# Prompt attention: causal masks taken from TensorE to VectorE and GpSimd

## Chip, cores and metric

The kernel runs on one core of one Trainium2 chip, as one program. The metric is the device time of that program in microseconds (us). Before the change it is 3462.72 us, the median of three runs (3456.31, 3462.72 and 3465.65 us).

## What is computed

One step of a two-layer streaming encoder on 1024 new frames of a prompt and on 8 x 16 frames of running streams with a cache of 2048 frames. The change touches the prompt's attention alone. Cut to that, the reference is:

```python
CHUNK = 64; QBLK = 128; DA_HEADS = 4; SB_HEADS = 8; HEAD_DIM = 64

def diff_attn_block(q, k, v, q_pos, k_pos, lam):
    s = jnp.einsum('bqhmd,bkhmd->mbhqk', q, k).astype(jnp.float32) * (HEAD_DIM ** -0.5)
    mask = (k_pos[None, :] // CHUNK) <= (q_pos[:, None] // CHUNK)
    p = jax.nn.softmax(jnp.where(mask, s, NEG_INF), axis=-1)
    w = p[0] - lam * p[1]
    return jnp.einsum('bhqk,bkhe->bqhe', w.astype(v.dtype), v)

def sb_attn_block(q, k, v, q_pos, k_pos):
    z = jnp.einsum('bqhd,bkhd->bhqk', q, k).astype(jnp.float32) * (HEAD_DIM ** -0.5)
    mask = k_pos[None, :] < q_pos[:, None]
    log_fail = jnp.where(mask, jax.nn.log_sigmoid(-z), 0.0)
    after = lax.cumsum(log_fail, axis=3, reverse=True) - log_fail
    a = jnp.where(mask, jnp.exp(jax.nn.log_sigmoid(z) + after), 0.0)
    return jnp.einsum('bhqk,bkhd->bqhd', a.astype(v.dtype), v)

for blk in range(t // QBLK):          # the prompt: 8 blocks of 128 queries, keys up to the block's end
    lo, hi = blk * QBLK, (blk + 1) * QBLK
    outs.append(fn(q[:, lo:hi], k[:, :hi], v[:, :hi], pos[lo:hi], pos[:hi], *extra))
```

All of it is float32. Only the last 128 x 128 block of keys of each query block needs a mask. For differential attention that is one quadrant: queries 0 to 63 must not see keys 64 to 127. For stick-breaking attention it is the triangle on and above the diagonal.

## The kernel before

The program is a row of phases for each of two layers: projection (with the cached streams' attention), prompt attention (`phase_attention`, prefix `B_`), merge (`D_`), and at the end a final norm. Each phase is written by hand for five engines. An engine has one in-order list of instructions, and semaphores tie the lists together. There is no scheduler: the lists follow one table of steps, `attention_steps()` (L617), which every engine goes through, picking what is its own.

`phase_attention` loops four times (h = 1..4) over pairs of heads of 128 columns; I call one turn a head. A turn has 16 items, n = 0..15: items 0 to 7 are differential attention (DA) and items 8 to 15 stick-breaking (SB), each for one block of 128 queries. An item with b = n % 8 + 1 blocks of keys computes, for m = 0 and 1 (the two maps of DA, the two heads of SB), 128 x 128b scores.

The order of the steps around item n is: `weights(n)`, `scores(n+1, 0)`, `functions(n+1, 0)`, `scores(n+1, 1)`, `functions(n+1, 1)`, `values(n-1)`, `out(n-1)`, then the rounds `prob_t(n)`. In detail:

- Scores (TensorE, L810): b x 128 columns in matmuls of up to 512, 64 rows deep, into PSUM tile `B_sc[:, m]`. Then a mask matmul (L812) adds, as identity times mask, 1e30 to the masked places of the last block. q was scaled by -1/8 beforehand, so a large positive number means masked. The mask matmul ends the group and tells `qk_done`.
- DA: VectorE takes the minimum (L904, `max_ready`), ScalarE the exponential with its sum into `B_ew` (L872, `s_free`), VectorE combines the two maps (L915 to L918, `weights_ready`).
- SB: ScalarE writes sigmoid(z) to `B_fun` (L878) and sigmoid(-z) to `B_ew` (L879, `s_free`). VectorE runs a backward product scan of `B_fun` into `B_surv` (L930) and multiplies `B_ew` by it (L931, `weights_ready`), for u = 0 and then u = 1. `B_fun` has one buffer per u, so the sigmoids of item n+1 wait for the product of item n of the same u.
- `prob_t`: TensorE transposes the weights (L789) in rounds of up to four blocks into two PSUM banks, which ScalarE and VectorE empty in turn into `B_wt` (L856, L891). Values: TensorE multiplies (L831) and VectorE copies the result out (L939, L941).

GpSimd has nothing to do in this phase. The masks come from a constant tile that ScalarE turns into the matmul's type once a phase (L852). PE records of a float32 matmul come in two halves, so x4 at L810 is two matmuls.

## Time and profile before

| | |
|---|---|
| median of three runs | 3462.72 us |
| profiled execution, its own time | 3463.09 us |
| its span | 3461.3 us |
| TensorE matmul busy | 3097.3 us, 89% |
| VectorE busy | 1591.5 us, 46% |
| ScalarE busy | 895.7 us, 26% |
| GpSimd busy | 0.2 us |
| granted TensorE clock, mean | 0.864 of full |
| prompt attention, layers 1 and 2 | about 925 to 1466 us and 2636 to 3178 us |

A busy TensorE here means that records overlap in time, not that the array is at its peak; a granted clock of 0.5 is 1.2 GHz and of 1.0 is 2.4 GHz. The page cuts the span in 40 slices of 86.5 us. In its PEclk row the slices of prompt attention read 7, 6, 6, 7, 6, 6 and 7, 7, 7, 7, 7, 5 (with the edges of the neighbours), where the projection has mostly 9.

### The profile page before, as it was taken

How to read it: one execution, taken by the hardware profiler on the slowest of the kernel's cores; microseconds unless marked ns; L12 is line 12 of the kernel's file. 1: busy time of each engine (PE TensorE's matmuls, PEld its weight loads, DVE VectorE, ACT ScalarE, POOL GpSimd, SP SyncE). 2: the span in 40 equal slices, each digit the busy share in tenths (PEclk: the TensorE clock that was granted, in tenths of full speed). 3: DMA queues.
4: the chain of work that ended last, by engine and by line, in shares of the span. 5: the costliest groups of instructions: out<-in, count | busy, mean ns of one | idle time of the engine just before them, and what ended most of it. 6: DMA issues, size and time to landing. Idle time of an engine off the chain costs nothing. (4 is left out here: it accounts for less than half of the span.)

```text
span 3461.3 us, 52533 instructions
## 1 busy us (share of the span) xinstructions
PE 3097.3 (89%) x21296; PEld 2299.0 (66%) x21296; DVE 1591.5 (46%) x1999; ACT 895.7 (26%) x1537; POOL 0.2 (0%) x4
## 2 busy tenths in 40 slices
PE   4989999999899999879868999999998999997895
PEld 3767677776666656658656767767765666665684
DVE  3634344444154554564356333444432554654553
ACT  2212222222142332320031222222222332333101
POOL 0000000000000000000000000000000000000000
PEclk9999999999876676689989999999997775775898
DMA  6378786676201100054344778767742010012444
GB/s 216 110 242 292 259 296 212 226 239 207 90 28 38 31 28 25 19 202 133 113 148 163 260 260 281 258 221 247 235 154 74 27 46 23 27 28 89 153 145 158
DMA packets 315425, 519.46 MB, mean 150 GB/s; under 512 B 40224, under 2 KB 111008, under 8 KB 315168
## 3 DMA queue, kind: packets, MB, share of 16 engines
q1 hardware_dynamic: 315248, 516.89, 44.4%
q8 instruction: 137, 2.24, 0.3%
q14 instruction: 40, 0.33, 0.0%
HBM read 436.58 MB, written 84.93 MB: 151 GB/s over the span
## 5 line engine op out<-in xcount | busy, mean ns | idle before, releaser
L335 PE MATMUL A_acc<-A_w_hi,A_ht_hi 128*128 128x512 f32 x1728 | 721.5, 418 | 38.1 <-DVE A_w_lo L540 19.1
L335 PE MATMUL A_acc<-A_w_lo,A_ht_hi 128*128 128x512 f32 x1728 | 684.9, 396 | 0.0
L335 PE MATMUL A_acc<-A_w_hi,A_ht_lo 128*128 128x512 f32 x1728 | 683.9, 396 | 0.0
L810 PE MATMUL B_sc<-B_kt,B_qt 64*128 64x512 f32 (+3 forms) x768 | 443.0, 697 | 16.9 <-DVE B_kt L891 15.5
L335 PEld LDWEIGHTS A_acc<-A_w_hi,A_ht_hi 128*128 128x128 f32 x1728 | 331.1, 192 | 134.1 <-issue 26.8
L335 PEld LDWEIGHTS A_acc<-A_w_hi,A_ht_lo 128*128 128x128 f32 x1728 | 330.7, 191 | 74.2
L335 PEld LDWEIGHTS A_acc<-A_w_lo,A_ht_hi 128*128 128x128 f32 x1728 | 332.1, 192 | 57.7
L831 PE MATMUL B_ov<-B_nat_v,B_wt 128*128 128x64 f32 (+1 forms) x1728 | 322.9, 362 | 14.4 <-DVE B_wt L891 14.4
L555 DVE STREAM_TRANSPOSE A_kt<-A_kt 128x2048 f32<-128x2048 f32 x128 | 293.1, 2302 | 76.5 <-DMA A_kt<-in_cache_da_k 69.5
L831 PEld LDWEIGHTS B_ov<-B_nat_v,B_wt 128*128 128x128 f32 x1728 | 305.8, 272 | 20.8 <-issue 20.8
L810 PEld LDWEIGHTS B_sc<-B_kt,B_qt 64*128 64x128 f32 x768 | 163.9, 245 | 156.0 <-issue 137.5
L540 DVE TENSOR_TENSOR A_w_lo<-A_w_raw,A_w_hi 128x1024 fp32r<-128x1024 f32 x96 | 116.5, 1220 | 209.8 <-ACT A_w_hi L432 209.2
L440 ACT ACTIVATE A_stage<-A_acc 128x512 f32<-128x512 f32 x180 | 107.0, 595 | 408.9 <-PE A_acc L335 282.2
L789 PE MATMUL B_tr<-ident,B_ew 128*128 128x128 f32 x864 | 176.8, 359 | 15.2 <-ACT B_wt L856 14.8
L930 DVE TENSOR_TENSOR_SCAN B_surv<-B_fun 128x255 f32<-128x255 f32 (+7 forms) x128 | 172.4, 1347 | 0.0
L482 ACT ACTIVATE A_pt<-A_tr 128x512 f32<-128x512 f32 x128 | 76.3, 596 | 371.6 <-PE A_tr L377 371.6
L812 PEld LDWEIGHTS B_sc<-B_masks_r 128*128 128x128 f32 x256 | 59.1, 231 | 163.8 <-issue 158.2
L432 ACT ACTIVATE A_w_hi<-A_w_raw 128x1024 fp32r<-128x1024 f32 x96 | 100.9, 1058 | 253.7 <-DMA A_w_raw<-in_w_in 138.5
L789 PEld LDWEIGHTS B_tr<-ident,B_ew 128*128 128x128 f32 x864 | 143.4, 194 | 27.3 <-ACT B_wt L856 25.4
L394 PE MATMUL A_ov<-A_v,A_pt 128*32 128x128 f32 x4096 | 140.1, 278 | 21.0 <-ACT A_pt L482 20.9
L872 ACT ACTIVATE B_ew<-B_sc,B_stats 128x256 f32<-128x256 f32 (+7 forms) x128 | 94.8, 740 | 238.5 <-DVE B_stats L904 238.5
L904 DVE TENSOR_REDUCE B_stats<-B_sc 128x1 f32<-128x256 f32 (+7 forms) x128 | 97.0, 758 | 126.7 <-PE B_sc L812 125.3
(132 smaller groups left out, 3287.6 us busy)
## 6 DMA issues: line engine op xcount, KB each, us to landing
A_kt<-in_cache_da_k SPq DMA_DIRECT2D x64, 1024.0 KB, 10.8
A_v<-in_cache_da_v SPq DMA_DIRECT2D x64, 1024.0 KB, 5.8
A_kt<-in_cache_sb_k SPq DMA_DIRECT2D x64, 1024.0 KB, 11.4
A_v<-in_cache_sb_v SPq DMA_DIRECT2D x64, 1024.0 KB, 5.8
A_w_raw<-in_w_in SPq DMA_DIRECT2D x96, 512.0 KB, 4.6
tmp_gates<-A_stage SPq DMA_DIRECT2D x72, 256.0 KB, 4.3
D_gate<-tmp_gates SPq DMA_DIRECT2D x72, 256.0 KB, 3.5
D_w_raw<-in_w_merge SPq DMA_DIRECT2D x32, 512.0 KB, 6.1
```

What stands on the lines that cost most here:

```text
L335: last = nc.tensor.matmul(acc[:, n % 2, :], h[:, k, rows], w[:, slot, cols], start=(k == 0 and j == 0), stop=(k == KC - 1 and j == 2))
L394: last = nc.tensor.matmul(ov[32 * c:32 * c + 32, 0:P], pt[:, slot, j, 32 * c:32 * c + 32], v_in[:, slot, j, c * P:(c + 1) * P], start=Fals ...
L432: nc.scalar.activation(w_hi[:, n % WSLOTS, :], w_raw[:, n % 2, :], ACT.Copy).then_inc(S["w_hi_done"], 1)
L440: ins = nc.scalar.activation(stage[:, n % 2, :], acc[:, n % 2, :], ACT.Sigmoid if gate else ACT.Copy)
L540: nc.vector.tensor_tensor(w_lo[:, n % WSLOTS, :], w_raw[:, n % 2, :], w_hi[:, n % WSLOTS, :].bitcast(F32), ALU.subtract).then_inc(S["w_lo_ ...
L555: nc.vector.transpose(keys, keys).then_inc(S["key_turned"], 1)
L789: last = nc.tensor.transpose(tr[:, r % 2, j * P:(j + 1) * P], block_, ident[:, :])
L810: nc.tensor.matmul(sc[:, m, c:e], qkt[0][m * HD:(m + 1) * HD, qb * P:(qb + 1) * P], qkt[1][m * HD:(m + 1) * HD, c:e], start=True, stop=(e ...
L831: last = nc.tensor.matmul(ov[:, cols], wt[:, u, j * P:(j + 1) * P], nat_v[a][:, j, cols], start=(j == 0), stop=(j == qb))
L872: nc.scalar.activation(e, z, ACT.Exp, scale=-1.0, bias=stats[n % 2][:, m:m + 1], accum_out=stats[n % 2][:, 2 + m:3 + m]).then_inc(S["s_fre ...
L904: nc.vector.tensor_reduce(out=stats[n % 2][:, m:m + 1], in_=sc[:, m, 0:(n + 1) * P], axis=AX.X, op=ALU.min)\
L930: step_(nc.vector.tensor_tensor_scan(out_, in_, in_, 1.0, ALU.mult, ALU.bypass))
```

## The change

The mask matmuls are gone. The last scores matmul of an item tells `qk_done` itself. In DA, VectorE first writes +1e30 into the masked quadrant of PSUM (64 partitions x 64 columns) and waits for its own write before it takes the minimum. In SB, the sigmoids are computed unmasked; GpSimd then sets the masked triangle of `B_fun` to 1 and of `B_ew` to 0 with one `affine_select` each, in place, on 128 x 128, and tells `masked`, on which the scan now waits in place of `s_free`. Also, the loops over h, `Fori` loops of the engines before, are now Python loops: the four heads are written out one after the other, and semaphore values are constants.

```diff
-        masks_r = sbuf("B_masks_r", [P, MASKS], F32R)
-        DSTEPS = 2 * NP_T + 2 * NP_T
+        DSTEPS = 2 * NP_T + 2 * NP_T + 2 * NP_T
...
             def _(pe):
-                pe.wait_ge(S["masks_ready"], 1)
-
-                with pe.Fori(1, NC + 1) as h:
+                for h in range(1, NC + 1):
...
-                                nc.tensor.matmul(sc[:, m, c:e], qkt[0][m * HD:(m + 1) * HD, qb * P:(qb + 1) * P],
-                                                 qkt[1][m * HD:(m + 1) * HD, c:e], start=True, stop=(e < keys))
-                            nc.tensor.matmul(sc[:, m, qb * P:keys], ident_r, mask_r[a], start=False, stop=True).then_inc(S["qk_done"], 1)
+                                last = nc.tensor.matmul(sc[:, m, c:e], qkt[0][m * HD:(m + 1) * HD, qb * P:(qb + 1) * P],
+                                                 qkt[1][m * HD:(m + 1) * HD, c:e], start=True, stop=True)
+                            last.then_inc(S["qk_done"], 1)
...
-                                nc.scalar.activation(fun[:, m, 0:keys], z, ACT.Sigmoid)
+                                nc.scalar.activation(fun[:, m, 0:keys], z, ACT.Sigmoid).then_inc(S["raw_ready"], 1)
                                 nc.scalar.activation(e, z, ACT.Sigmoid, scale=-1.0).then_inc(S["s_free"], 1)
+            @block.gpsimd
+            def _(pool):
+                def before_me(tile, fill):
+                    return nc.gpsimd.affine_select(out=tile, in_=tile, pattern=[[-1, P]], compare_op=ALU.is_gt, fill=fill,
+                                                   base=0, channel_multiplier=1)
+                for h in range(1, NC + 1):
+                    for step in STEPS:
+                        if step[0] == "functions" and step[1] >= NP_T:
+                            _, n, m = step
+                            diag = slice((n - NP_T) * P, (n - NP_T + 1) * P)
+                            pool.wait_ge(S["raw_ready"], h * (2 * NP_T) + (2 * (n - NP_T) + m + 1))
+                            before_me(fun[:, m, diag], 1.0)
+                            pool.wait_ge(S["s_free"], h * (2 * ITEMS) + (2 * n + m + 1))
+                            before_me(ew[n % 2][:, m, diag], 0.0).then_inc(S["masked"], 1)
...
                             dve.wait_ge(S["qk_done"], h * (2 * ITEMS) + (2 * n + m + 1))
+                            step_(nc.vector.memset(sc[0:CHUNK, m, n * P + CHUNK:(n + 1) * P], -NEG))
                             nc.vector.tensor_reduce(out=stats[n % 2][:, m:m + 1], in_=sc[:, m, 0:(n + 1) * P], axis=AX.X, op=ALU.min)\
...
-                                    dve.wait_ge(S["s_free"], h * (2 * ITEMS) + (2 * n + u + 1))
+                                    dve.wait_ge(S["masked"], h * (2 * NP_T) + (2 * (n - NP_T) + u + 1))
```

On TensorE, in the second half of a turn, the order around the scores of the SB item with six blocks of keys was this (`B_tr` are transposes, `B_ov` the values):

```order
L810 MATMUL B_sc<-B_kt,B_qt 128x512
L810 MATMUL B_sc<-B_kt,B_qt 128x256
L812 MATMUL B_sc<-B_masks_r 128x128
L807 REGISTER_ALU
L810 MATMUL B_sc<-B_kt,B_qt 128x512
L810 MATMUL B_sc<-B_kt,B_qt 128x256
L812 MATMUL B_sc<-B_masks_r 128x128
L723 REGISTER_ALU
L825 REGISTER_ALU
L831 MATMUL B_ov<-B_nat_v,B_wt 128x64 x8
L789 MATMUL B_tr<-ident,B_ew 128x128 x5
L723 REGISTER_ALU
L789 MATMUL B_tr<-ident,B_ew 128x128 x5
```

And now TensorE has, at the same place:

```order
L805 MATMUL B_sc<-B_kt,B_qt 128x512
L805 MATMUL B_sc<-B_kt,B_qt 128x256
L805 MATMUL B_sc<-B_kt,B_qt 128x512
L805 MATMUL B_sc<-B_kt,B_qt 128x256
L826 MATMUL B_ov<-B_nat_v,B_wt 128x64 x8
L784 MATMUL B_tr<-ident,B_ew 128x128 x10
```

Nothing has changed places: the mask matmuls and the register instructions are gone, and the second map's scores are followed at once by the values.

On VectorE, at the start of a turn (DA item 0), there stood before:

```order
L903 REGISTER_ALU
L904 TENSOR_REDUCE B_stats<-B_sc 128x1
L903 REGISTER_ALU
L904 TENSOR_REDUCE B_stats<-B_sc 128x1
L914 ISA
L915 RECIPROCAL B_stats<-B_stats 128x2
```

And now, at the same place:

```order
L914 MEMSET B_sc 64x64
L915 TENSOR_REDUCE B_stats<-B_sc 128x1
L914 MEMSET B_sc 64x64
L915 TENSOR_REDUCE B_stats<-B_sc 128x1
L926 RECIPROCAL B_stats<-B_stats 128x2
L927 SCALAR_TENSOR_TENSOR B_stats<-B_stats,nlam 128x1
```

Each minimum has got a write of PSUM ahead of it. GpSimd, which had nothing in the phase, now has this for SB (`B0_` marks layer 1's semaphores):

```order
L877 ISA [waits B0_raw_ready]
L877 AFFINE_SELECT B_fun<-B_fun 128x128
L877 AFFINE_SELECT B_ew<-B_ew 128x128 [waits B0_s_free]
L877 AFFINE_SELECT B_fun<-B_fun 128x128 [waits B0_raw_ready]
L877 AFFINE_SELECT B_ew<-B_ew 128x128 [waits B0_s_free]
```

Four selects an item stand there, the two of u = 0 ahead of the two of u = 1.

## Rows read from the trace of the kernel before

**Rows 1.** Windows: length, busy of PE, PEld, DVE, ACT, POOL; granted clock; DMA, GB/s

```profile
925.00:1466.00 541.00, 506.34 (x1936) 341.03 (x1936) 281.41 (x441) 184.44 (x353) 0.00 (x0) 0.67 0.11 31
2600.00:3180.00 580.00, 535.72 (x2127) 364.41 (x2125) 282.26 (x444) 189.90 (x361) 0.00 (x0) 0.69 0.12 34
```

**Rows 2.** Groups by line, 925 to 1466; busy us, mean ns, idle before and releasers

```profile
L812 PE MATMUL B_sc<-B_masks_r 128*128 128x128 f32 x128 | 50.4, 394 | 0.0
...
L904 DVE TENSOR_REDUCE B_stats<-B_sc 128x1 f32<-128x128 f32 (+7 forms) x64 | 48.5, 758 | 63.9 <-PE B_sc L812 63.4
```

**Rows 3.** Timeline at half clock: start us, us, instruction, idle before it and releaser

```profile
946.48 0.47 PE L812 MATMUL B_sc<-B_masks_r 128*128 128x128 f32 x1
946.88 2.07 PE L810 MATMUL B_sc<-B_kt,B_qt 64*128 64x512 f32 x2
...
948.89 0.47 PE L812 MATMUL B_sc<-B_masks_r 128*128 128x128 f32 x1
949.05 0.97 PEld L831 LDWEIGHTS B_ov<-B_nat_v,B_wt 128*128 128x128 f32 x4
```

**Rows 4.** Timeline at full clock, the same places of a later item

```profile
969.84 0.33 PE L812 MATMUL B_sc<-B_masks_r 128*128 128x128 f32 x1
...
970.10 1.77 PE L810 MATMUL B_sc<-B_kt,B_qt 64*128 64x512 f32 x4
...
971.79 0.33 PE L812 MATMUL B_sc<-B_masks_r 128*128 128x128 f32 x1
971.90 1.20 PEld L831 LDWEIGHTS B_ov<-B_nat_v,B_wt 128*128 128x128 f32 x10
```

**Rows 5.** Windows of one turn, cut where the granted clock changes

```profile
968.00:1012.40 44.40, 40.78 (x220) 27.11 (x218) 31.36 (x52) 22.54 (x44) 0.00 (x0) 1.00 0.17 50
1012.40:1067.00 54.60, 52.34 (x186) 39.60 (x187) 23.54 (x24) 12.54 (x18) 0.00 (x0) 0.50 0.02 5
1067.00:1070.40 3.40, 2.23 (x11) 1.38 (x9) 1.28 (x3) 2.30 (x6) 0.00 (x0) 1.00 0.44 131
1070.40:1101.10 30.70, 30.70 (x72) 16.94 (x71) 14.16 (x31) 8.60 (x24) 0.00 (x0) 0.50 0.16 43
```

**Rows 6.** Timeline, VectorE in DA: a memset, and a minimum at full clock

```profile
925.20 0.06 DVE L883 MEMSET B_surv<- 128x2 f32 x1 [25.68 <-PEq L63]
...
974.94 1.15 DVE L918 SCALAR_TENSOR_TENSOR B_ew<-B_ew,B_stats 128x896 f32<-128x896 f32 x1
...
976.15 1.23 DVE L904 TENSOR_REDUCE B_stats<-B_sc 128x1 f32<-128x1024 f32 x1
```

**Rows 7.** Timeline, VectorE and ScalarE in SB items 11 and 12, full clock

```profile
1000.38 1.21 DVE L930 TENSOR_TENSOR_SCAN B_surv<-B_fun 128x511 f32<-128x511 f32 x1
...
1002.23 1.22 DVE L930 TENSOR_TENSOR_SCAN B_surv<-B_fun 128x511 f32<-128x511 f32 x1
...
1003.08 0.70 ACT L879 ACTIVATE B_ew<-B_sc 128x640 f32<-128x640 f32 x1
...
1005.79 1.48 DVE L930 TENSOR_TENSOR_SCAN B_surv<-B_fun 128x639 f32<-128x639 f32 x1
```

**Rows 8.** Timeline, SB item 8: the shortest operations on 128 x 128

```profile
989.44 0.41 DVE L930 TENSOR_TENSOR_SCAN B_surv<-B_fun 128x127 f32<-128x127 f32 x1
```

**Rows 9.** Timeline: GpSimd's own instructions, one of four alike

```profile
0.24 0.10 POOL L1368 MEMSET const-float32-0.0<- 128x1 f32 x1 [0.24 <-issue]
```

**Rows 10.** Timeline, TensorE where the clock falls and at the next turn's start

```profile
1012.55 1.33 PE L789 MATMUL B_tr<-ident,B_ew 128*128 128x128 f32 x5 [1.59 <-ACT B_wt L856]
...
1063.76 1.91 PE L789 MATMUL B_tr<-ident,B_nat_q 128*128 128x128 f32 x8
```

**Rows 11.** Timeline, TensorE around the place where the clock rises

```profile
965.19 2.02 PE L831 MATMUL B_ov<-B_nat_v,B_wt 128*128 128x128 f32 x8
...
968.14 1.77 PE L810 MATMUL B_sc<-B_kt,B_qt 64*128 64x512 f32 x4
...
973.87 1.98 PE L810 MATMUL B_sc<-B_kt,B_qt 64*128 64x512 f32 x4
```

More of the change, by code:

```diff
@@ L681, in phase_attention @@
     with scope:
-        names = ["masks_ready", "surv_set", "turned", "f_a", "f_v",
+        names = ["surv_set", "turned", "f_a", "f_v", "raw_ready", "masked",
                  "qk_done", "max_ready", "s_free", "weights_ready", "pv_done", "o_ready", "dve_step",
@@ L701, in phase_attention @@
         ident, nlam = const["ident"], const["nlam"]
-        ident_r = masks_r[:, 0:P]
-        mask_r = [masks_r[:, P:2 * P], masks_r[:, 2 * P:3 * P]]
         v_nat_sems = [S["nat_v0"], S["nat_v1"]]
@@ L708, in phase_attention @@
         last_prob = {s[1]: s[-1] for s in STEPS if s[0] == "prob_t"}
-        DSTEPS = 2 * NP_T + 2 * NP_T
+        DSTEPS = 2 * NP_T + 2 * NP_T + 2 * NP_T
         start_phase(nc, [(S["turned"], ROUNDS)] + list(zip(F, COPIES))
-                    + [(S[k], 2 * ITEMS) for k in ("qk_done", "s_free", "weights_ready")] + [(S["max_ready"], 2 * NP_T)]
+                    + [(S[k], 2 * ITEMS) for k in ("qk_done", "s_free", "weights_ready")] + [(S[k], 2 * NP_T) for k in ("max_ready", "raw_ready", "masked")]
                     + [(S[k], ITEMS) for k in ("pv_done", "o_ready")]
@@ L738, in load_slice @@
                 def load_slice(h, dst, src, sem):
-                    cols = bass.ds(h * P - P, P)
+                    cols = slice(h * P - P, h * P)
                     sp.dma_start(dst[:, :, :], src[0:SEQ, cols].rearrange("(t p) c -> p t c", p=P)).then_inc(sem, 16)
@@ L761, in body @@
                             qb = n % NP_T
-                            cols = bass.ds(h * P - P, P)
+                            cols = slice(h * P - P, h * P)
                             sp.wait_ge(S["o_ready"], h * ITEMS + (n + 1))
@@ L770, in _ @@
                 load_slice(1, nat_v[0], dram["v_da"][l], v_nat_sems[0])
-                with sp.Fori(1, NC) as h:
+                for h in range(1, NC):
                     body(h, False)
@@ L851, in _ @@
             def _(act):
-                nc.scalar.activation(masks_r[:, :], const["masks"][:, :], ACT.Copy).then_inc(S["masks_ready"], 1)
-                with act.Fori(1, NC + 1) as h:
+                for h in range(1, NC + 1):
                     def copy(dst, src, scale=None):
@@ L877, in _ @@
                                 act.wait_ge(S["qk_done"], h * (2 * ITEMS) + (2 * n + m + 1))
-                                nc.scalar.activation(fun[:, m, 0:keys], z, ACT.Sigmoid)
+                                nc.scalar.activation(fun[:, m, 0:keys], z, ACT.Sigmoid).then_inc(S["raw_ready"], 1)
                                 nc.scalar.activation(e, z, ACT.Sigmoid, scale=-1.0).then_inc(S["s_free"], 1)
+            @block.gpsimd
[3 more added lines that the diff above has]
+                                                   base=0, channel_multiplier=1)
+                for h in range(1, NC + 1):
+                    for step in STEPS:
[6 more added lines that the diff above has]
+                            before_me(ew[n % 2][:, m, diag], 0.0).then_inc(S["masked"], 1)
             @block.vector
@@ L884, in _ @@
                 dve.wait_ge(S["surv_set"], 1)
-                with dve.Fori(1, NC + 1) as h:
+                for h in range(1, NC + 1):
                     step_ = Steps(dve, S["dve_step"], h * DSTEPS - DSTEPS)
```

## The prediction, made before the changed kernel ran

> **What bounds the kernel now.** I read the windows first, to see which stages the change can reach. Prompt attention is about 541 us in each layer, and in both the TensorE is busy for over nine tenths of it, at a mean granted clock of 0.67 and 0.69 where VectorE is busy for only half [rows 1]. Then I read the groups by line. In layer 1 the 128 mask matmuls have 50.4 us of busy time, with no idle before them; the minimum of DA sat idle for 63.4 us on L812 [rows 2]. So TensorE's list is the spine of the phase, and other engines wait for it. The page's chain of waits ends in the final norm and says nothing of this phase. Third, I cut one turn where the granted clock changes [rows 5]. It is at 2.4 GHz (1.00) for 44.4 us, at 1.2 GHz (0.50) for 54.6, at 2.4 for 3.4 and at 1.2 for 30.7: together 133.1 us, of which 85.3 at the half clock. There TensorE is busy for 52.3 of 54.6 and 30.70 of 30.70 us, and VectorE for less than half. At the full clock VectorE is busy for 31.4 of 44.4 us, and with ScalarE it holds TensorE up at times. The reader should see two regimes: at half clock only TensorE counts; at full clock TensorE, VectorE and ScalarE are nearly level.
>
> **What TensorE is relieved of.** There are 16 items a turn with two masks each, four turns and two layers: 256 mask matmuls. The busy time of one (0.47 us at half clock) includes its latency, so I take the distance between starts. Behind the first map's scores, the mask pushes the next scores back by 946.88 - 946.48 = 0.40 us at half clock [rows 3] and 970.10 - 969.84 = 0.26 at full clock [rows 4]. Behind the second map's, the weight load of the values starts 949.05 - 948.89 = 0.16 us after the mask, and 0.11 at full clock [rows 3, 4]; without the mask it can start where the mask did. One item thus gives 0.56 us at half clock and 0.37 at full clock. In the timeline of the turn, 9 items have their masks at full clock (the first, the last two of DA and the first six of SB) and 7 at half clock (five of DA, the last two of SB). The ceiling is 7 x 0.56 + 9 x 0.37 = 7.25 us a turn, 58 us in eight turns.
>
> **Half clock: all of it is kept.** 7 x 0.56 x 8 = 31 us. VectorE gets two memsets in each of the DA items there. Before, the minimum waited for the mask to end; now it is released a mask earlier and does a memset first. The trace has no write of 64 x 64 to PSUM. From below there is the memset of 2 columns, 0.06 us [rows 6]; from above VectorE's scan of 127 columns, 0.41 us [rows 8]. I take 0.15, nearer the memset, and 0.05 for the wait on its own write, so 0.2 against the 0.4 that the mask took: the exponentials come a little sooner, and nothing is lost. If TensorE did not hold the pace, this cover would be gone, as in the next part.
>
> **Full clock, DA.** The minimum over 1024 columns at 976.15 has no idle before it: VectorE had just finished the product that started at 974.94 and took 1.15 us [rows 6]. With two memsets (0.4 us) on a VectorE that is the later one, the last DA item gives nothing. The one before it had idle time on VectorE and gives its 0.37: 3 us in eight turns. The first item of a turn is a chain of short waits and gives nothing.
>
> **Full clock, SB.** The first two SB items have little for VectorE to do, and TensorE carries the values of DA beside them: 2 x 0.37 x 8 = 6 us. From the third to the sixth, VectorE's round and TensorE's are level: from the scan at 1000.38 to that at 1005.79 is 5.4 us [rows 7], in which scan, product, scan, product, two copies and the wait for the last transposes follow each other. Relief for TensorE gives nothing there. Are the selects late? Sigmoid(-z) of u = 0 ends at 1003.08 + 0.70 = 1003.78, its scan starts at 1005.79 [rows 7]: 2.0 us for at most two selects, and for u = 1 there is as much. What a select takes, no row shows. From below there is GpSimd's memset of one column, 0.10 us [rows 9]. From above I take VectorE's minimum over 1024 columns, eight times the elements: 1.23 us [rows 6]. I take 0.4, from the scan of 127 columns [rows 8]. With 0.4 `masked` comes in time. But the selects do not run beside an idle VectorE. The select on `B_fun` of the next item becomes ready just before 1003.08, in this item's second scan (1002.23 to 1003.45 in item 11), and GpSimd and VectorE then both stream from SBUF. Nothing here shows whether one of them waits. If not, the cost is 0; if VectorE's next instruction waits for one select per map, it is 0.8 us an item. I take half of that, 0.4 us, for four items a turn: 4 x 0.4 x 8 = 13 us lost.
>
> The Trainium skill speaks against the change at this point. "SBUF — State Buffer", section "Who interferes with whom", says that a VectorE instruction with two SBUF inputs and a GpSimd instruction that reads SBUF exclude each other for a whole instruction, whoever started first. The scan and the product here are such instructions; no trace of before can show it, for GpSimd idles. By that rule the cost would be the full 0.8 us an item, 26 us in place of 13.
>
> **Loops and the rest.** The removed loops save a jump and register instructions per turn. TensorE starts the next turn's transposes at 1063.76 [rows 10] while its last values are still draining, so I take 0. The skill's "Runtime: NRT & Kernel Launch", section "Instruction fetch mechanics", would have a taken branch stall on a fetch; TensorE's rows here show no such gap, and by them the sum stays. `masks_r` saves ScalarE one 0.5 us copy per layer, under the wait for the first loads. Projection, merge and final norm are not touched.
>
> **Sum.** 31 + 3 + 6 - 13 = 27 us. The profiled execution took 3463.1 us for a span of 3461.3, and is 0.4 above the median of the runs, so I take 3463.1 - 27 = 3436 us.
>
> **What the sum leaves to chance: where the clock changes.** The clock falls at 1012.4, just as TensorE resumes after 1.59 us of waiting for ScalarE's copy [rows 10]. It rises at 968.0 after a run of values and transposes (from 965.19), where the scores (64 rows deep) had gone before [rows 11]. In each later turn it rises at the same place of the work. Without masks these runs are 0.3 us shorter at half clock and lie elsewhere in time. If the rise comes one item later, the item from 968.14 to 973.87, 5.7 us long, costs up to twice as much.
>
> **Rivals.**
> 1. The clock rises one item late in most turns. [...] Price: 5.2 us less 0.2 for masks dearer there, 5.0 a turn, 40 in eight: 3476 us. If it happens in half the turns, 3456.
> 2. Slower: the selects hold VectorE up. One mechanism, in SB items 3 to 6 at full clock: each item's chain gets two select lengths. With the upper bound of 1.23 us that is 4 x 2 x 1.23 x 8 = 79 us, and the 6 us of the first two SB items are gone too: 3463.1 - 34 + 79 = 3508. It decides from 34 / 64 = 0.53 us a select. For it: every scan waits behind them. Against it: a select has 128 elements per partition, and the row of that size takes 0.41 us [rows 8]. This is also what the skill's rule on SBUF, cited above, would do if a select is long.
> 3. More is gained: selects and scans don't disturb each other, TensorE's relief counts fully at full clock, and the clock falls later. 58 us: 3405 us.
> 4. The masks were hidden all along and nothing changes: 3463 us. For it: TensorE records overlap. Against it: rows 3 show the next start pushed back.
>
> **How the numbers follow.** My forecast, including half of rival 1 and up to the full 0.8 us an item: 0.56, with its own range 3420 to 3456. Rival 1: 0.14. Rival 2: 0.13, mostly under 3508. Rival 3: 0.12. Rival 4: 0.05. For this kernel no change means within 0.3%, 10.4 us, of the median, so 3452.3 to 3473.1. Faster: 0.53 of the forecast's share, all of rival 3, none of the others, 0.65. Same: 0.03 of the forecast, rival 4, most of rival 1 if it is milder than priced, 0.09: together 0.17. Slower: rival 2 and 0.05 of rival 1: 0.18. The range from 3400 to 3480 leaves out most of rival 2 and the edges.
>
> **What would show it.** In the profile after: no second group of matmuls on `B_sc`; scores and values follow at 0.1 us. The AFFINE_SELECT rows' mean: under 0.5 us keeps the sum, above it rival 2. Idle time of the product or scan with releaser POOL in SB tells whether VectorE waits for selects, and a longer mean of the scan that it is slowed. The full-clock stretch of a turn: 44 us as now, or near 38 for rival 1. A turn of 133.1 us should become about 129.7. The forecast is wrong if the memset waits on something longer than its own write (0.2 us), or if the granted clock in prompt attention leaves 0.64 to 0.70.

## The result

| | before | after |
|---|---|---|
| device time, median (range) | 3459.51 us (3450.04 to 3465.65), 4 runs | 3246.38 us (3242.20 to 3249.15), 4 runs |
| profiled execution, its own time and span | 3463.09 / 3461.3 us | 3244.39 / 3242.6 us |
| prompt attention, layers 1 and 2 | 538.7 + 537.5 us | 426.5 + 430.7 us |
| of it at the half clock | 350.9 + 346.3 us | 152.2 + 164.5 us |
| projection, both layers | 915.0 + 910.2 us | 916.5 + 908.1 us |
| merge, both layers | 249.5 + 251.1 us | 251.0 + 249.2 us |

The change makes the kernel 6.15% faster: the ratio is 0.9385, with a 95% interval from 0.9359 to 0.9411. That is 213 us. I had forecast 27 us, with a range down to 3400 us. The prediction was wrong by far, though its sign was right. All of the gain lies in prompt attention: 112.2 + 106.8 = 219 us between the two profiled executions, whose spans are 218.7 apart. (The phases are cut at their first and last record in the trace, the two clock rows add up the stretches at 1.2 GHz inside them.)

From the page of the changed kernel, the busy time of the engines and the clock row:

```profile
PE 2774.6 (86%) x21040; PEld 2118.6 (65%) x21040; DVE 1599.5 (49%) x2127; ACT 890.7 (27%) x1535; POOL 114.0 (4%) x260
PEclk9989999999987988789989999999999878986998
```

Windows of prompt attention in both layers, then of one turn, cut where its clock changes for long (length, busy of PE, PEld, DVE, ACT and POOL, granted clock, DMA):

```profile
925.00:1403.00 478.00, 371.81 (x1912) 272.39 (x1913) 315.78 (x546) 199.92 (x374) 57.15 (x128) 0.81 0.20 59
2525.00:2957.00 432.00, 346.32 (x1808) 252.85 (x1808) 285.39 (x505) 181.83 (x352) 56.69 (x128) 0.81 0.14 40
...
1142.40:1164.30 21.90, 18.02 (x58) 11.70 (x58) 12.31 (x37) 7.87 (x21) 0.00 (x0) 0.50 0.30 82
1164.30:1212.10 47.80, 38.87 (x231) 27.18 (x229) 36.69 (x68) 26.29 (x52) 9.84 (x24) 1.00 0.17 47
1212.10:1249.10 37.00, 30.64 (x168) 24.80 (x169) 22.29 (x22) 11.31 (x16) 4.62 (x8) 0.73 0.02 6
```

The first window takes in 50 us of the merge behind the phase, as the second of [rows 1] takes in 36 us ahead of it; over the phases alone, cut as in the table, the granted clock is 0.82 and 0.81 where it was 0.67 and 0.68. Two things stand out against [rows 1, 5]. One is that clock. The other is that a turn of 106.7 us has 47.8 at the full clock (44.4 before), then 37.0 in which the clock goes up and down at a mean of 0.73, where it stood at 0.50 for 54.6 us. TensorE is now busy for 39 of the 48 us at the full clock: it waits more, and it does not hold the others up as it did.

The place of [rows 3] in the changed kernel, on TensorE at the half clock (start, length, instruction). These are the scores of the DA item with four blocks of keys:

```profile
944.51 2.72 PE L805 MATMUL B_sc<-B_kt,B_qt 64*128 64x512 f32 x4
947.16 0.58 PE L826 MATMUL B_ov<-B_nat_v,B_wt 128*128 128x128 f32 x1
```

And of the kernel before, the two ends of the same place that [rows 3] leave out:

```profile
944.48 2.07 PE L810 MATMUL B_sc<-B_kt,B_qt 64*128 64x512 f32 x2
949.16 0.52 PE L831 MATMUL B_ov<-B_nat_v,B_wt 128*128 128x128 f32 x1
```

The changed kernel's first row explains the result. Before, the first map's matmul began at 944.48, its mask at 946.48, the second map at 946.88, its mask at 948.89 [rows 3], and the values at 949.16: 4.68 us. Now both maps take 947.16 - 944.51 = 2.65 us, at the same clock. Two masks and two gaps can't be 2 us. Each map alone took 2.00 us before (944.48 to 946.48); both together now take 2.65. They run side by side. The trace's single records say the same. This is how many of L805's are under way in two stretches, the second of which begins where the second map does (length, busy of PE and of the weight load with records, granted clock, DMA):

```profile
944.60:945.15 0.55, 0.55 (x1) 0.41 (x2) 0.50 0.00 0
945.15:945.30 0.15, 0.15 (x2) 0.14 (x1) 0.50 0.00 0
```

The first half of the first map's matmul runs to 945.73, and the second map starts in the midst of it, at 945.16. The kernel before has one record (x1) of L810 in either stretch.

Groups by line of the changed kernel, 925 to 1403 (busy us, mean ns, idle before and releasers):

```profile
L805 PE MATMUL B_sc<-B_kt,B_qt 64*128 64x512 f32 (+3 forms) x384 | 128.9, 635 | 24.8 <-ACT B_ew L866 16.0 <-issue 3.6 <-ACT B_kt L850 3.6
L941 DVE TENSOR_TENSOR_SCAN B_surv<-B_fun 128x127 f32<-128x127 f32 (+7 forms) x64 | 86.8, 1356 | 0.5 <-POOL B_ew L877 0.2
L784 PE MATMUL B_tr<-ident,B_ew 128*128 128x128 f32 x432 | 75.7, 312 | 37.7 <-ACT B_wt L850 30.1 <-DVE B_ew L942 7.3
L915 DVE TENSOR_REDUCE B_stats<-B_sc 128x1 f32<-128x128 f32 (+7 forms) x64 | 48.5, 758 | 2.2
L866 ACT ACTIVATE B_ew<-B_sc,B_stats 128x128 f32<-128x128 f32 (+7 forms) x64 | 47.4, 740 | 66.3 <-DVE B_stats L915 63.5 <-PE B_tr L784 1.7
L877 POOL TENSOR_SCALAR_AFFINE_SELECT B_fun<-B_fun 128x128 f32<-128x128 f32 x64 | 23.5, 367 | 1269.1 <-ACT B_fun L872 1268.8
L914 DVE MEMSET B_sc<- 64x64 f32 x64 | 7.2, 112 | 8.3 <-PE B_sc L805 7.7
```

VectorE's wait for the scores in DA was 63.4 us [rows 2] and is 7.7 (it is the memset that waits now). The selects cost VectorE 0.2 us of waiting. TensorE, which had no large wait there, now waits 30.1 us for ScalarE's copy and 16.0 for its exponential.

### The profile page after: what moved, and what is told of

The parts are those of the page before. It is cut to its first block and busy times, and to the rows that moved or that the text cites. A ratio compares the mean times of both kernels' runs of the same rounds, so it can differ in the third digit from the quotient of the medians.

```text
span 3242.6 us, 50812 instructions
## 1 busy us (share of the span) xinstructions
PE 2774.6 (86%) x21040; PEld 2118.6 (65%) x21040; DVE 1599.5 (49%) x2127; ACT 890.7 (27%) x1535; POOL 114.0 (4%) x260
## 5 line engine op out<-in xcount | busy, mean ns | idle before, releaser
L805 PE MATMUL B_sc<-B_kt,B_qt 64*128 64x512 f32 (+3 forms) x768 | 257.9, 637 | 49.1 <-ACT B_ew L866 31.7
L826 PEld LDWEIGHTS B_ov<-B_nat_v,B_wt 128*128 128x128 f32 x1728 | 241.2, 222 | 86.2 <-issue 61.0
L826 PE MATMUL B_ov<-B_nat_v,B_wt 128*128 128x64 f32 (+1 forms) x1728 | 264.2, 313 | 13.3 <-ACT B_wt L850 9.7
L784 PE MATMUL B_tr<-ident,B_ew 128*128 128x128 f32 x864 | 152.4, 314 | 76.9 <-ACT B_wt L850 61.7
L805 PEld LDWEIGHTS B_sc<-B_kt,B_qt 64*128 64x128 f32 x768 | 121.2, 228 | 133.2 <-issue 67.8
L784 PEld LDWEIGHTS B_tr<-ident,B_ew 128*128 128x128 f32 x864 | 116.5, 165 | 98.1 <-issue 69.5
L941 DVE TENSOR_TENSOR_SCAN B_surv<-B_fun 128x255 f32<-128x255 f32 (+7 forms) x128 | 173.5, 1356 | 1.0 <-POOL B_ew L877 0.2
L394 PEld LDWEIGHTS A_ov<-A_v,A_pt 128*32 128x32 f32 x4096 | 105.4, 110 | 71.2 <-issue 45.1
L354 PE MATMUL A_csc<-A_kt,A_qkt 32*32 32x512 f32 x4096 | 143.7, 597 | 1.6 <-issue 1.5
L877 POOL TENSOR_SCALAR_AFFINE_SELECT B_fun<-B_fun 128x128 f32<-128x128 f32 x128 | 46.4, 362 | 2804.4 <-ACT B_fun L872 2803.8
```

The lines of the kernel that those rows point to most:

```text
L354: last = nc.tensor.matmul(csc[32 * c:32 * c + 32, b, :], qkt[quad, 0, o:o + 32], kt[quad, :, o:o + 32], start=(d == 0), stop=(d == 3))
L394: last = nc.tensor.matmul(ov[32 * c:32 * c + 32, 0:P], pt[:, slot, j, 32 * c:32 * c + 32], v_in[:, slot, j, c * P:(c + 1) * P], start=Fals ...
L784: last = nc.tensor.transpose(tr[:, r % 2, j * P:(j + 1) * P], block_, ident[:, :])
L805: last = nc.tensor.matmul(sc[:, m, c:e], qkt[0][m * HD:(m + 1) * HD, qb * P:(qb + 1) * P], qkt[1][m * HD:(m + 1) * HD, c:e], start=True, s ...
L826: last = nc.tensor.matmul(ov[:, cols], wt[:, u, j * P:(j + 1) * P], nat_v[a][:, j, cols], start=(j == 0), stop=(j == qb))
L941: step_(nc.vector.tensor_tensor_scan(out_, in_, in_, 1.0, ALU.mult, ALU.bypass))
```

## The experiments

Three theories stand in the expectations. A: the two maps' scores use the array rows 0 to 63 and 64 to 127 (64*128 in the records; q and k of map m lie in partitions 64m to 64m + 63), and overlap once nothing of full height stands between them. D: the granted clock follows the shape of the work in time, and an edit that shifts it can move tens of microseconds. E, later, is that a sigmoid in ScalarE's way holds up TensorE. Beside these stand the plainer ones: the masks' own time, the loops, the selects. Each run has its own runs of the kernel before beside it; the ratio is to them.

**The loops alone.** In the kernel before, on SyncE, TensorE, ScalarE and VectorE:

```diff
-                with pe.Fori(1, NC + 1) as h:
+                for h in range(1, NC + 1):
```

> The kernel before with its four-head loops of prompt attention written out, masks untouched. Theory A (without a full-height mask matmul between them, the scores of the two maps, one in the upper and one in the lower 64 rows of the array, run side by side): no change, 3450 to 3470 us, and a turn stays at 133 us. Theory B (written-out loops are what helped): most of the 213 us comes here, below 3350 us.

Measured: 3391.21 us, 0.9825 (0.9764 to 0.9885). Prompt attention in layer 1 is in the window

```profile
925.00:1437.00 512.00, 453.69 (x1936) 302.10 (x1936) 281.11 (x440) 184.46 (x353) 0.00 (x0) 0.77 0.12 34
```

The matmul records are as many as in [rows 1] (x1936), and at the same clock they last as long as before (a record of the values has a mean of 0.43 us at the half and 0.28 at the full clock in both); but the clock is 0.77 and not 0.67. So writing out the loops gave 60 us, give or take 20, through the clock alone. That is too little for the result, and its sign does not carry over, as the last two runs show.

**The changed kernel, with the second map held back** until the first one's scores are done:

```diff
+                            if m == 1:
+                                pe.wait_ge(S["qk_done"], h * (2 * ITEMS) + (2 * n + 1))
```

> The changed kernel with one wait more: on TensorE the second map's scores wait until the first map's are complete (qk_done). No mask matmul comes back. Theory A: the overlap is gone and so is most of the gain; what stays is what I forecast for the masks' own time, less the wait of 0.1 to 0.2 us per item: 3400 to 3450 us. Theory C (the masks' own time, their weight loads and their latency ahead of the minimum were simply far dearer than I priced): the waits cost 128 x 0.2 = 26 us at most, 3250 to 3275 us.

Measured: 3441.69 us (3380.35 to 3457.15), against 3448.91 for before beside it. It varied too much from run to run for a ratio; all of its runs are well above the 3246 us of the changed kernel. The same scores took

```profile
949.74 4.26 PE L807 MATMUL B_sc<-B_kt,B_qt 64*128 64x512 f32 x4
953.94 0.58 PE L828 MATMUL B_ov<-B_nat_v,B_wt 128*128 128x128 f32 x1
```

4.20 us. The masks are gone here, and the median is only 7 us below that of before. But the edit also adds a wait, so the next but one does the same without one.

**The kernel before, its masks behind both maps.** No matmul is removed; the order is scores, scores, mask, mask:

```diff
-                            nc.tensor.matmul(sc[:, m, qb * P:keys], ident_r, mask_r[a], start=False, stop=True).then_inc(S["qk_done"], 1)
+                            if m == 1:
+                                for mm in range(2):
+                                    nc.tensor.matmul(sc[:, mm, qb * P:keys], ident_r, mask_r[a], start=False, stop=True).then_inc(S["qk_done"], 1)
```

> The kernel before, all 256 mask matmuls kept on TensorE and nothing on GpSimd, but in another order: scores of both maps first, then both masks. Theory A: the scores overlap, and most of the gain comes without removing any mask: 3246 plus at most my 58 us for the masks' own time, 3270 to 3330 us, and the granted clock in prompt attention rises from 0.67 to about 0.78. Theory C: the masks still cost what they cost, 3440 to 3470 us.

Measured: 3255.04 us (3249.52 to 3264.92), 0.9438 (0.9402 to 0.9475). Swapping two instructions gives 194 us with all 256 mask matmuls kept. At the half clock:

```profile
937.09 2.63 PE L810 MATMUL B_sc<-B_kt,B_qt 64*128 64x512 f32 x4 [0.18 <-ACT B_ew L874]
939.66 0.69 PE L814 MATMUL B_sc<-B_masks_r 128*128 128x128 f32 x2
940.14 0.52 PE L833 MATMUL B_ov<-B_nat_v,B_wt 128*128 128x128 f32 x1
```

3.05 us from the first score to the values, of which the two masks have 940.14 - 939.66 = 0.48. Of the 4.68 us before, 1.63 came from the place of the first mask, and not from its work. (The 194 us hold what the shorter scores did to the clock also: 0.82 and 0.78 in the two layers here.)

**The changed kernel, both maps from the same rows.** The second map is computed from the first map's rows:

```diff
-                                last = nc.tensor.matmul(sc[:, m, c:e], qkt[0][m * HD:(m + 1) * HD, qb * P:(qb + 1) * P],
-                                                 qkt[1][m * HD:(m + 1) * HD, c:e], start=True, stop=True)
+                                last = nc.tensor.matmul(sc[:, m, c:e], qkt[0][0:HD, qb * P:(qb + 1) * P],
+                                                 qkt[1][0:HD, c:e], start=True, stop=True)
```

> The changed kernel, except that the second map's scores are computed from the first map's rows (partitions 0 to 63 of q and k, for both). The number, shapes and order of all instructions and waits stay; the output of the second maps is not the reference's. Theory A (the two maps overlap because they sit in different halves of the array's rows): the overlap is gone, the scores of four blocks at half clock take about 2 x 2.0 = 4.0 us again in place of 2.65, and the time is 3380 to 3450 us. Theory C (what counted was the mask matmul itself and the switch of type and height around it): no change, 3240 to 3255 us.

Measured: 3425.73 us, 0.9895 (0.9862 to 0.9928). The instructions, their order and every wait are those of the changed kernel; only the partitions of the second map's operands differ, and with them the rows of the array, and 179 us are gone. (Its second maps are not the reference's.) The same place:

```profile
944.95 3.78 PE L805 MATMUL B_sc<-B_kt,B_qt 64*128 64x512 f32 x4
948.66 0.79 PE L826 MATMUL B_ov<-B_nat_v,B_wt 128*128 128x128 f32 x2
```

3.71 us, nearly twice the 2.00 of one map alone, in place of 2.65. This settles theory A in what it says of the time. Whether the array's rows or the reading of the operands' partitions is what the two maps then have to share, no run can tell, since the one goes with the other. The run also says what the change would have been worth without the overlap: 36 us, with 11 either way; the one with the second map held back, which adds a wait, gives 7.

**The changed kernel, the two maps interleaved.** With more than four blocks of keys a map is two matmuls; here they alternate between the maps, and both maps' buffers are waited for ahead of the first:

```diff
-                            pe.wait_ge(S["s_free"], h * (2 * ITEMS) + (2 * n + m - 1))
+                            if m == 0:
+                                continue
+                            pe.wait_ge(S["s_free"], h * (2 * ITEMS) + 2 * n)
...
+                                for mm in range(2):
+                                    last = nc.tensor.matmul(sc[:, mm, c:e], qkt[0][mm * HD:(mm + 1) * HD, qb * P:(qb + 1) * P],
+                                                            qkt[1][mm * HD:(mm + 1) * HD, c:e], start=True, stop=True)
...
```

> The changed kernel with the scores of the two maps issued chunk by chunk in turn (first map's first 512 keys, second map's first 512 keys, then the rest of both) in place of all of one map and then all of the other. It changes only items with more than 512 keys. Theory A: there only the middle part overlaps now, and with b = 8 blocks three chunks' time would become two, 0.85 us less per item at full clock and 1.7 at half clock; 64 such items, of which perhaps half are bound by TensorE: 3190 to 3225 us. Theory C: the amount of work on TensorE is the same, 3240 to 3252 us.

Measured: 3274.25 us (3264.60 to 3286.70), 0.9500 (0.9459 to 0.9542): slower than the changed kernel, against the expectation. The scores themselves are shorter, as theory A says: 2.01 us at the place of the 2.65, and for the three last DA items, at the full clock, 1.49, 1.70 and 1.92 against 2.40, 2.75 and 3.09. What it cost is in its waits (who waits for whom, us, times, longest) and in the first row's bracket:

```profile
950.28 2.08 PE L808 MATMUL B_sc<-B_kt,B_qt 64*128 64x512 f32 x4 [1.10 <-ACT B_ew L870]
952.29 1.01 PE L830 MATMUL B_ov<-B_nat_v,B_wt 128*128 128x128 f32 x3
```

```profile
PE B_sc L808 <- ACT B_ew L870: 40.7, 28, 2.7
```

At four blocks a map is a single matmul, so there the order is that of the changed kernel, and what differs is when the second map may start. In the changed kernel that is when ScalarE is done with its PSUM buffer, that is, with the exponential of the item before (its last record, then the weight load of the second map):

```profile
944.91 0.19 ACT L866 ACTIVATION_READ_ACCUMULATOR B_ew<-B_sc,B_stats 128x1 f32 x1
945.16 0.28 PEld L805 LDWEIGHTS B_sc<-B_kt,B_qt 64*128 64x128 f32 x1
```

ScalarE ends at 945.10, and the second map starts at 945.16, 0.65 us after the first. That is the whole of 2.65 - 2.01: with both buffers free, the two maps start together. TensorE waits 40.7 us in layer 1 before scores, where the changed kernel waits 16.0, since it may no longer start the first map while ScalarE still reads the second. The overlap gained 0.6 to 1.2 us an item, and waits took it all and more.

**The changed kernel without its selects.**

```diff
-            @block.gpsimd
-            def _(pool):
...
-                            before_me(fun[:, m, diag], 1.0)
...
-                            before_me(ew[n % 2][:, m, diag], 0.0).then_inc(S["masked"], 1)
...
-                                    dve.wait_ge(S["masked"], h * (2 * NP_T) + (2 * (n - NP_T) + u + 1))
+                                    dve.wait_ge(S["s_free"], h * (2 * ITEMS) + (2 * n + u + 1))
```

> The changed kernel without the 256 selects on GpSimd; the scans wait for s_free as before, and the triangle of stick-breaking attention is left unmasked, so its output is not the reference's. It prices the selects. If VectorE waits for them for one select per map and item at full clock, as the forecast had it (0.4 us for 4 items a turn, and more of the time is at full clock now), 13 to 30 us are saved: 3215 to 3233 us. If the selects wait for VectorE and not the other way round, as the 1.0 to 1.3 us long selects next to scans of 0.95 and 1.21 us suggest: 3238 to 3250 us, no change.

Measured: 3244.73 us (3239.01 to 3257.64), 0.9389 (0.9354 to 0.9423), against 0.9385 for the changed kernel. The selects cost nothing that can be measured. By the interval alone that could hide some 12 us, nearly what I had forecast; the traces narrow it. Over items 11 and 12 the scans are 5.22 us apart with the selects and without, and the mean of a scan is 1356 ns with them and 1347 without: 1 us for all 128.

**More work in the kernel before.** Four extra transposes at the start of each turn, into a tile that is then overwritten:

```diff
+                            if (a, which, half) == (0, 0, 0):
+                                for _ in range(4):
+                                    nc.tensor.transpose(tr[:, r % 2, 0:P], nat[0][:, 0, :], ident[:, :])
```

> The kernel before with four more 128 x 128 transposes at the start of each of the eight turns, whose result is overwritten. As work they are 4 x 0.11 us at full or 4 x 0.22 us at half clock, 4 to 7 us in all. Theory D (the loops' 58 us in the first group of runs came from nothing but where in the work the granted clock changes): the time moves by more than that work, in either direction, by up to 60 us; a turn's length in the profile is no longer 133.1 us. Without theory D: 3452 to 3460 us, 4 to 7 us above before.

Measured: 3377.32 us (3365.22 to 3420.49), 0.9759 (0.9715 to 0.9804). With more to do it is 84 us faster. One turn of before and the same turn here:

```profile
1063.70:1197.00 133.30, 126.25 (x487) 85.16 (x487) 70.34 (x110) 45.98 (x88) 0.00 (x0) 0.68 0.12 31
```

```profile
1047.40:1163.40 116.00, 105.63 (x490) 71.57 (x490) 70.31 (x110) 45.65 (x88) 0.00 (x0) 0.84 0.13 36
```

VectorE and ScalarE are busy for the same time. TensorE does the same and a little more in 17 us less, at 0.84 against 0.68. That is theory D by itself, without any of the change's parts. The two layers show how loosely: with the same instructions, prompt attention takes 473 us in layer 1 and 514 in layer 2, of 539 and 538 before.

**The changed kernel, a later sigmoid.** TensorE's wait for ScalarE's copy is the largest one left, so I put the second sigmoids of the next SB item behind this item's transposes on every engine's list:

```diff
-                add("functions", n + 1, m)
+                if m == 0 or n < NP_T:
+                    add("functions", n + 1, m)
...
+        if NP_T <= n < ITEMS - 1:
+            add("functions", n + 1, 1)
```

> The changed kernel with one step moved: in stick-breaking items ScalarE computes the sigmoids of the next item's second map behind its copies of this item's transposed weights, not ahead of them. In the changed kernel's profile TensorE waits 2 to 3 us an item there for ScalarE, whose copy stands behind sigmoids that wait for VectorE's product (PE B_tr L784 waited 37.8 us for ACT B_wt L850 in layer 1). Theory E (at full clock the items are now bound by that ring of VectorE, ScalarE and TensorE, and not by TensorE's work): 25 to 70 us are gained, 3175 to 3220 us, and the full clock lasts longer in the second half of a turn. Its rival (TensorE's work still bounds): 3240 to 3250 us.

Measured: 3241.31 us (3229.94 to 3248.54), 0.9362 (0.9325 to 0.9398): the same as the changed kernel within the spread, and above what was expected. The wait moved. Its SB item with seven blocks shows

```profile
1209.03 1.77 PE L808 MATMUL B_sc<-B_kt,B_qt 64*128 64x512 f32 x4
1211.42 1.77 PE L808 MATMUL B_sc<-B_kt,B_qt 64*128 64x512 f32 x4 [0.62 <-ACT B_ew L876]
1213.11 3.14 PE L829 MATMUL B_ov<-B_nat_v,B_wt 128*128 128x64 f32 x16
```

In the items with seven and eight blocks the second map now comes after a wait for the later sigmoid, and the two no longer overlap: 4.08 us here, where the changed kernel has 2.68. One part of theory E did come: prompt attention has 277 us at the half clock in place of 317. It brought no time.

**Masks and loops apart.** Four kernels make a square: masks on TensorE but behind, or off it; loops kept or written out. First the changed kernel with loops on four engines (GpSimd's list stays written out):

```diff
-                for h in range(1, NC + 1):
+                with pe.Fori(1, NC + 1) as h:
```

> The changed kernel with the loops over h restored on SyncE, TensorE, ScalarE and VectorE (GpSimd's list stays written out). It is the mask change alone. Theory A (the gain comes from the two maps' scores running side by side in the two halves of the rows, with the clock higher for longer because the half-clock work is done sooner): the loops add nothing of their own, time 3240 to 3265 us, scores of both maps from start to start as in the changed kernel. Theory L (the written-out loops gave a share of their own, since writing them out alone gave 58 us): 3265 to 3305 us, with the difference where the granted clock falls, not in segments at equal clock.

Measured: 3229.33 us (3208.75 to 3231.47), 0.9339 (0.9317 to 0.9361). Then the kernel with the masks behind, loops written out:

```diff
-                with pe.Fori(1, NC + 1) as h:
+                for h in range(1, NC + 1):
...
+                            if m == 1:
+                                for mm in range(2):
...
```

> The kernel before with each item's two mask matmuls moved behind the scores of both maps, and the loops written out. The masks stay on TensorE, so against the changed kernel only the 256 mask matmuls remain. Theory A: as with the loops kept (3255 us), or less by a few us, 3240 to 3260; the masks' own cost (0.4 us an item at half clock, 0.25 at full) is 10 to 25 us at most. Theory L: the loops give their share here also, 3200 to 3235 us, faster than the changed kernel.

Measured: 3276.07 us (3274.94 to 3280.86), 0.9479 (0.9457 to 0.9502). I had written 3240 to 3265 and 3240 to 3260 for theory A, and more or less for theory L; neither expected that loops are the faster ones. So I ran the changed kernel and its version with loops once more, beside each other on one chip.

> The changed kernel once more, beside the next run on the same chip. Theory L2 (with the scores side by side, written-out loops cost about 17 us, as e9 against the changed kernel and e10 against e3 suggest): 3240 to 3252 us, and 12 to 22 us over the next run. Theory N (the 17 us are the spread between measurements): within 5 us of the next run.

> The changed kernel with the loops restored on four engines, once more. Theory L2: 3222 to 3236 us. Theory N: 3232 to 3250, within 5 us of the run before it.

Measured: 3247.18 us (3242.21 to 3252.74), 0.9401 (0.9388 to 0.9415), and 3222.38 us (3220.45 to 3224.11), 0.9330 (0.9318 to 0.9343). The difference is 25 us, and the kernel with the new masks and the old loops is the fastest of the four. Prompt attention in layer 1, of the changed kernel and of this one:

```profile
933.00:1363.00 430.00, 345.27 (x1808) 251.29 (x1808) 285.59 (x505) 181.78 (x352) 56.99 (x128) 0.81 0.14 40
```

```profile
923.00:1341.00 418.00, 338.34 (x1808) 247.25 (x1808) 285.05 (x505) 182.09 (x352) 59.03 (x128) 0.83 0.15 40
```

The same 1808 matmul records, 12 us less, a clock 0.02 higher. Over both layers, prompt attention has 328 us at the half clock in the changed kernel and 309 with loops. Between the two profiled executions, whose spans are 28.5 us apart, prompt attention accounts for 14.6 us, and the projections, which no edit touches, for 12.9. What moved the projections is open; I only see that it was so in the first pair too (17.7 and 14.3 of 35.6). A rival that no run tests is the fetching of instructions, of which a written-out kernel has more: the instruction queue carries 158 packets in the changed kernel and 136 with loops. It was 160 against 137 in the kernel before, where writing out the loops made it faster.

As ratios, with loops the masks on TensorE cost 0.9438 - 0.9330 = 0.0108, 37 us, and without loops 0.9479 - 0.9401 = 0.0078, 27 us, each with some 10 us either way and with its share of the clock in it. Writing out the loops changes before by -60 us, the kernel with masks behind by +14 (0.0041; the two were measured on different runs of before, and their intervals overlap, so this middle one may be nothing) and the changed kernel by +25.

## Why the prediction was wrong

**The step that failed** is "One item thus gives 0.56 us at half clock and 0.37 at full clock". It priced the mask by how far it pushes back what comes after it. It took for granted that the scores behind it could start no sooner than the mask's own place. They can: without a matmul of 128 rows between them, the second map's matmul, in rows 64 to 127, runs beside the first one's, in rows 0 to 63. At the place that I had read, an item gives 4.68 - 2.65 = 2.03 us, not 0.56, and the ceiling of 58 us was none. The kernel with the masks behind shows it with no work removed (194 us), and the one with both maps in the same rows takes it away with nothing added (179 us). The trace of before could not show the overlap, for a mask stood behind every map. But it had the premise: scores of 64*128 next to a mask of 128*128 in [rows 3], and a kernel that addresses `m * HD:(m + 1) * HD`. I read "64 rows deep" and took it for a thin use of the array, not for half of it being free.

The Trainium skill, which I had not weighed on this point, has the rule: "TensorEngine Tiling (Array Packing)", section "Key Properties", says that tiles of the array work independently, and that different tiles can load weights and multiply in parallel. The trace agrees, with 2.65 us against 3.71 in the same rows.

**The clock.** I wrote that a granted clock outside 0.64 to 0.70 would make the forecast wrong; it is 0.82 and 0.81. The half clock's share of prompt attention fell from 697 to 317 us, of a total that fell by 219. The two gains can't be added up, since the shorter scores are also what changed the pattern of the clock. But one number separates some of it. The values are the same instructions before and after; in the timeline, from their start to the next start, they take 285 us of both layers before and 235 after. (The last row of each layer, which has no next start, is left out.) Less than 1 us of either is waiting, and at the same clock a record of them lasts as long as before within 0.01 us, so these 50 us come from the clock. The scores went from 496 to 268 us by the overlap, the masks and the clock together; transposes with the waits behind them grew from 272 to 335, all of it waiting. That is 496 + 285 + 272 = 1053 against 838, a difference of 215. My paragraph on chance looked at a single outcome, a rise that comes one item late. The 5.2 us that priced it stand in no row; the item it names is 5.7 us long. The runs show tens of microseconds in both directions: four transposes more gave -84, writing out the loops gave -60 in one kernel and +25 in another.

**Half clock, 31 us, and the other parts of the sum.** Counted as I counted, without the overlap, the gain was about right: masks off TensorE, there with the overlap in both kernels, gave 27 and 37 us in the square above, and the kernel with both maps in the same rows is 36 us faster than before, loops included, against a sum of 27. That the 27 is close is partly luck: it has 13 us for selects that cost nothing, and edits that only shift the clock's changes moved the time by more than that.

**The memset** was near: 0.15 us and 0.05 for the wait. In the changed kernel, VectorE at a late DA item:

```profile
964.83 1.15 DVE L929 SCALAR_TENSOR_TENSOR B_ew<-B_ew,B_stats 128x896 f32<-128x896 f32 x1
965.99 0.11 DVE L914 MEMSET B_sc<- 64x64 f32 x1
966.13 1.22 DVE L915 TENSOR_REDUCE B_stats<-B_sc 128x1 f32<-128x1024 f32 x1
```

It takes 0.11 us, and the minimum starts 966.13 - 965.99 = 0.14 after it. As predicted, VectorE has no idle time here [rows 6], so the last DA items pay it.

**The selects, -13 us.** The size was right, 0.4 us: their means in layer 1 are 0.367 us on `B_fun` and 0.544 on `B_ew`, the second above the 0.5 that I had named as the sign of rival 2, which did not come. What I got wrong is who waits. GpSimd's and VectorE's rows in the changed kernel, first with the scan ahead or level, then with the select 0.02 us ahead:

```profile
988.01 0.29 POOL L877 TENSOR_SCALAR_AFFINE_SELECT B_fun<-B_fun 128x128 f32<-128x128 f32 x1 [0.62 <-ACT B_fun L872]
...
988.42 1.21 DVE L941 TENSOR_TENSOR_SCAN B_surv<-B_fun 128x511 f32<-128x511 f32 x1
988.42 1.30 POOL L877 TENSOR_SCALAR_AFFINE_SELECT B_ew<-B_ew 128x128 f32<-128x128 f32 x1
...
993.62 0.29 POOL L877 TENSOR_SCALAR_AFFINE_SELECT B_ew<-B_ew 128x128 f32<-128x128 f32 x1 [0.22 <-ACT B_ew L873]
993.64 1.60 DVE L941 TENSOR_TENSOR_SCAN B_surv<-B_fun 128x639 f32<-128x639 f32 x1
```

Alone, a select takes 0.29 us. Started with the scan, it took 1.30 and ended 0.09 after it, while the scan took its usual 1.21 [rows 7]. Where the select was first, the scan took 1.60 us in place of 1.48 [rows 7]. That is what two instructions would show that exclude each other; but where it costs much, the long scan runs and the short select waits, on an engine that nobody needs yet. The rule of the Trainium skill that the prediction cited ("SBUF — State Buffer", section "Who interferes with whom") is borne out in kind, and the 26 us that I had it cost are not: the run without selects is as fast within its spread.

**Full clock.** In SB the step held. From scan to scan over items 11 and 12 is 993.64 - 988.42 = 5.22 us, against 5.41 [rows 7]: TensorE's gain turns into waits there, as it should where the ring of VectorE and ScalarE sets the pace. With the overlap this reached further than I had it. From the first scan of the item with six blocks to that of the item with seven it was 14.85 us before, at the half clock, with TensorE busy for 14.59. It is 9.08 now at a mean clock of 0.88, and 9.09 in the kernel before with written-out loops, at the full clock there. My premise that at the half clock only TensorE counts held for the kernel before and not for the changed one. That interleaving did not pay fits this, though no run shows it by itself.

**The rivals.** The one that came nearest, "more is gained", had the right sign, an end of 3405 us, and no mechanism for more. Rival 2 fell with the selects. My signs to look for worked where the mechanism was known; the turn of 133.1 us became 106.7, not 129.7, and the full-clock stretch of a turn is 47.8 us, so rival 1 did not come.

## What to carry to other kernels

Before pricing a matmul by its own time, look at the rows that its neighbours use. Here two matmuls of 64 rows lay in different halves, and the one of full height between them cost their overlap also; moving such a one behind both can be worth more than removing it (here 194 us against 27 to 37). And where the granted clock changes inside a stage, a few per cent of a time can come from edits that should do nothing: test the parts of a change apart, and both ways, before one of them gets the credit.

## What the runs showed of the hardware

- Two matmuls of 64 x 512, at the half clock, four records: 3.71 us when both are in the same rows; 2.65 in different rows, where the second starts 0.65 us late because its buffer is still being read; 2.01 in different rows with both buffers free. No mode or position was set in the kernel's code; the partitions of the operands were enough.
- Nothing of the overlap is left with a matmul of 128 rows between the two: 4.68 us with two masks, against 3.05 with both masks behind.
- A select of 128 x 128 float32 on GpSimd takes 0.29 us alone and took 1.30 beside a scan of VectorE; a memset of 64 x 64 in PSUM on VectorE takes 0.11 us.
- The clock was granted fully for longer in a kernel with four more transposes a turn (0.84 against 0.68 over a turn of layer 1). What exactly decides it was not settled here.
